# A hybrid decoder step on one core: the expert routing by pairs of heads, and the output projection by blocks of its inputs

## The reference

```python
z = rmsnorm(x, norm1_g) @ w_in                     # 2048 -> 6200
y_a = cb * short_conv(cc * ch)                     # columns    0..511  of the mixer output
y_b = gated sum of three attention branches        # columns  512..1535
y_c = gated, normed mLSTM heads (4 x 128)          # columns 1536..2047
x = x + concat(y_a, y_b, y_c) @ w_out              # 2048 -> 2048
h = rmsnorm(x, norm2_g)
q = (h @ wq).reshape(T, 8, 2, 128)                 # 8 heads, two halves
s = einsum('thcd,hcnd->thcn', q, subkeys)          # 16 sets of 128 scores a row
s1, i1 = top_k(s[:, :, 0], 16); s2, i2 = top_k(s[:, :, 1], 16)
top, pos = top_k(s1[..., :, None] + s2[..., None, :], 16)    # of 256 candidates a head
eidx = i1 * 128 + i2 at pos;  g = softmax(top)
act = gelu(einsum('td,thkd->thk', h, u[eidx]))     # 128 gathered rows of u a token
x = x + einsum('thk,thkd->td', g * act, v[eidx])   # 128 gathered rows of v a token
y = rmsnorm(x, final_norm_g)
```

## Time and profile before

| | |
|---|---|
| median of 3 runs | 3102.96 us (3099.08 to 3103.07) |
| the profiled execution | 3101.28 us, span 3099.5 us |
| busy in the span | PE 1612.3 us (52%), DVE 2002.9 (65%), POOL 1096.2 (35%), ACT 270.3 (9%) |
| mean granted PE clock | 0.707 of full |
| moved by DMA | 992.93 MB, of these 671.13 by gathers |
| gathers, 640 | 10.3 us (u) and 16.3 us (v) from issue to landing, medians |

### The profile page before, as it was taken

One profiled execution on the slowest core, in us unless ns is written; L12 is line 12 of the kernel. 1 busy time (PEld: TensorE's weight loads), 2 busy tenths in 40 slices (PEclk: granted clock), 3 DMA queues, 4 the chain that ended last, 5 costly groups with the idle time before them and its releaser, 6 DMA issues.

```text
span 3099.5 us, 20042 instructions
## 1 busy us (share of the span) xinstructions
PE 1612.3 (52%) x6113; PEld 1010.5 (33%) x6113; DVE 2002.9 (65%) x2607; ACT 270.3 (9%) x590; POOL 1096.2 (35%) x644
## 2 busy tenths in 40 slices
PE   7985956778887756632767667424787000000000
PEld 3454552222224632632545555301277000000000
DVE  0024147766664864663777777676562999999998
ACT  1012101000001200100211111200010000000000
POOL 0000003233440222201334334222430488888885
PEclk9975987899897568766888878755855555555555
DMA  8942748999994669837899999866994599999997
GB/s 275 304 147 82 260 141 317 414 412 412 412 412 139 244 220 394 346 96 285 346 387 387 388 392 401 301 192 216 396 402 196 226 422 422 422 422 422 422 422 320
DMA packets 267343, 992.93 MB, mean 320 GB/s; under 512 B 31218, under 2 KB 60599, under 8 KB 183433
## 3 DMA queue, kind: packets, MB, share of 16 engines
q0 software_dynamic: 92160, 671.13, 53.2%
q1 hardware_dynamic: 174072, 319.40, 29.5%
q10 hardware_dynamic: 1040, 1.59, 0.1%
HBM read 980.73 MB, written 19.77 MB: 323 GB/s over the span
## 4 chain that ended last, share of the span: by engine, by line
PE 36%; DMA 24%; POOL 16%; DVE 13%; issue 5%; SPq 4%; ACT 2%; DVEq 0%; ACTq 0%; POOLq 0%
POOL arena L1584 16%; PE ps L724 10%; DMA arena<-in_w_in_dram 10%; PE ps L865 6%; DMA arena<-in_cache_nsa_kv_dram 6%; PE ps L843 5%; DMA arena<-in_w_out_dram 3%; PE ps L360 2%; DMA arena<-in_peer_wq_dram 2%; SPq L565 2%; SPq L566 2%; PE ps L363 2%; DVE arena L1072 2%; DMA arena<-in_peer_v_dram,arena 2%; DVE arena L1150 1%
## 5 line engine op out<-in xcount | busy, mean ns | idle before, releaser
L1584 POOL DMA_INDIRECT arena<-in_peer_u_dram,arena x320 | 496.7, 1552 | 1373.4 <-DVEq L1533 705.8
L1069 DVE CUSTOM_DVE_ANT_0 arena<-arena 128x2048 bf16<-128x2048 f32 x320 | 733.4, 2292 | 241.5 <-DMA arena<-in_peer_u_dram,arena 183.2
L1584 POOL DMA_INDIRECT arena<-in_peer_v_dram,arena x320 | 599.3, 1873 | 599.4 <-DVE arena L1072 385.2
L1072 DVE SCALAR_TENSOR_TENSOR arena<-arena 128x2048 f32<-128x2048 f32 x296 | 696.0, 2351 | 102.4 <-DMA arena<-in_peer_v_dram,arena 63.5
L724 PE MATMUL ps<-arena 128*128 128x512 f32 (+1 forms) x1152 | 544.7, 629 | 78.9 <-DMA arena<-in_w_in_dram 76.7
L724 PEld LDWEIGHTS ps<-arena 128*128 128x128 f32 (+1 forms) x1152 | 202.4, 183 | 420.0 <-issue 316.9
L865 PE MATMUL ps<-arena 128*128 128x128 f32 (+1 forms) x1536 | 236.3, 334 | 32.7 <-DMA arena<-in_peer_wq_dram 32.7
L865 PEld LDWEIGHTS ps<-arena 128*128 128x128 f32 x1536 | 235.1, 249 | 33.9 <-DMA arena<-in_peer_wq_dram 22.3
L843 PE MATMUL ps<-arena 128*128 128x512 f32 (+1 forms) x384 | 189.7, 656 | 53.5 <-DMA arena<-in_w_out_dram 53.5
L360 PE MATMUL ps<-arena 128*128 128x128 f32 x512 | 74.8, 319 | 193.1 <-DMA arena<-in_cache_nsa_kv_dram 193.1
L360 PEld LDWEIGHTS ps<-arena 128*128 128x128 f32 x512 | 73.3, 234 | 196.0 <-DMA arena<-in_cache_nsa_kv_dram 196.0
(11 more groups left out here) (327 smaller groups left out, 1607.7 us busy)
## 6 DMA issues: line engine op xcount, KB each, us to landing
arena<-in_w_in_dram SPq DMA_DIRECT2D x96, 1024.0 KB, 8.7
arena<-in_w_out_dram SPq DMA_DIRECT2D x48, 1024.0 KB, 10.2
arena<-in_peer_wq_dram SPq DMA_DIRECT2D x48, 1024.0 KB, 5.7
arena<-in_cache_nsa_kv_dram SPq DMA_DIRECT2D x128, 384.0 KB, 9.0
arena<-in_cache_nsa_kv_dram SPq DMA_DIRECT2D x128, 128.0 KB
arena<-in_state_win_kv_dram SPq DMA_DIRECT2D x32, 256.0 KB, 21.7
out_s_win_dram<-in_state_win_kv_dram SPq DMA_DIRECT2D x1, 8064.0 KB
arena<-in_peer_u_dram,arena POOLq DMA_INDIRECT x320, 10.3
```

The source lines that it names most:

```text
L1069: nc.vector.tensor_tensor_reduce(out=PROD, in0=rows_in, in1=H[t], scale=1.0, scalar=0.0, op0=ALU.mult, op1=ALU.add, accum_out=DOTS[:, c:c ...
L1072: nc.vector.scalar_tensor_tensor(out=ACC[t], in0=rows_in, scalar=GG[:, t, c:c + 1], in1=ACC[t], op0=ALU.mult, op1=ALU.add).then_inc(g_used, 1)
L1584: nc.gpsimd.indirect_dma_start(BUF[SLOT[p]], None, tables[kind], bass.IndirectOffsetOnAxis(EIDX[:, t, c:c + 1].bitcast(U32), 0)).then_inc( ...
```

## The change

Two things, in one diff.

**The output projection by blocks of its inputs.** `out_part(n)` multiplies input block `Y_ORDER[n // 4]` (1, 2, 0, 3: attention, attention, convolution, heads) into column block n % 4. All four column blocks stay open in PSUM banks 4 to 7 until the last four parts. In tiles 0 and 1, the two attention blocks of Y are transposed when the attention ends, ACT copies them ahead of the forget gates, and their eight parts are issued two to a head: one behind the score matmuls, one behind the transposes of the weighted scores. SP issues 12 of the 16 loads in that order there, ahead of the stores of the mLSTM memory. Behind the heads stand two blocks' transposes and eight parts. Tile 2 has the new order, with all parts behind the heads. DVE's addition to x of column c now waits for part 12 + c.

**Routing by pairs of heads.** Column block c of the query projection holds two PEER heads, four score sets. The four 128-column groups of a block now share one bank, and one ACT copy takes them. After blocks 1, 2 and 3, PE computes the scores of the pair before (`pair_scores`), the last pair's follow; ACT stores them in two alternating buffers outside RING, and DVE routes each pair by itself (`route_pair`), every step a quarter as wide. In tiles 1 and 2 the 20 gathered rows ahead of the routing become 10, 4, 3 and 3, ahead of each pair. POOL waits for each pair's quarter of the row numbers. `v_cd` now comes after the last pair. Tile 1's and the sample's first norm move into tile 0's query projection and routing. For tile 2 the row numbers and gates of the two halves are laid out in another order.

```diff
+        Y_ORDER = (1, 2, 0, 3)
+        Y_BANK = (2, 3, 0, 1)
 ...
-                for n in range(4):
-                    sp.dma_start(RING[:, n], w_part(w_out, 0, n)).then_inc(w_slot[n], 16)
+                for n in range(12 if t < 2 else 4):
+                    if n >= 4:
+                        sp.wait_ge(w_used, W1[t] + n - 3)
+                    sp.dma_start(RING[:, n % 4], w_part(w_out, n % 4, Y_ORDER[n // 4])).then_inc(w_slot[n % 4], 16)
 ...
+                def out_part(n):
+                    i, c = n // 4, n % 4
+                    pe.wait_ge(a_yt, 4 * t + i + 1)
+                    pe.wait_ge(w_slot[c], 4 * W1[t] + 16 * i + 16)
+                    for j in range(KS):
+                        last = nc.tensor.matmul(ps[0:r, 4 + c, :], XT[:, KS * Y_ORDER[i] + j, 0:r], RING[:, c, j, :],
+                                                start=(i == 0 and j == 0), stop=(i == 3 and j == KS - 1))
+                    last.then_inc(w_used, 1)
+                if t < 2:
+                    pe.wait_ge(v_uy, NU * t + NU)
+                    for i in range(2):
+                        y_transposed(i)
 ...
                     nc.tensor.matmul(ps[0:r, 1, 0:w], MQT[:, h, 0:r], MKT[:, h, 0:w], start=True, stop=True).then_inc(t_gr, 1)
+                    if t < 2:
+                        out_part(2 * h)
                     pe.wait_ge(v_wqk, hh + 1)
 ...
                     last.then_inc(t_mwt, 1)
+                    if t < 2:
+                        out_part(2 * h + 1)
                     pe.wait_ge(a_mwt, hh + 1)
 ...
+                for i in range(2 if t < 2 else 0, 4):
+                    y_transposed(i)
+                for n in range(8 if t < 2 else 0, 16):
+                    out_part(n)
 ...
+                    if c:
+                        pair_scores(c - 1)
+                pair_scores(3)
 ...
+                def scores_out(c):
+                    act.wait_ge(t_sc, 4 * t + c + 1)
+                    if c >= 2:
+                        act.wait_ge(v_route, 4 * t + c - 1)
+                    nc.scalar.copy(SC[c % 2][r], ps[r, 6 + c % 2].rearrange("p (q n) -> p q n", q=4)).then_inc(a_sc, 1)
 ...
-                    dve.wait_ge(w_used, W1[t] + 4 * c + 4)
+                    dve.wait_ge(w_used, W1[t] + 12 + c + 1)
 ...
+                for c in range(4):
+                    if t:
+                        take((10, 4, 3, 3)[c])
+                    dve.wait_ge(a_sc, 4 * t + c + 1)
+                    route_pair(t, c)
+                    if t == 0 and c == 1:
+                        first_mean(1)
+                        first_mean(2)
+                    if t == 0 and c == 2:
+                        first_rstd(1)
+                        first_rstd(2)
 ...
-                if kind == "u" and c == 0:
-                    pool.wait_ge(v_route, t + 1)
+                if kind == "u" and c % (COLS[t] // 4) == 0:
+                    pool.wait_ge(v_route, 4 * t + c // (COLS[t] // 4) + 1)
```

More of the change, by code:

```diff
@@ L993, in _, with yt_stored @@
                     mlstm_qk()
+                def yt_stored(i):
+                    j = Y_ORDER[i]
+                    act.wait_ge(t_y, 4 * t + i + 1)
+                    nc.scalar.copy(XT[:, 4 * j:4 * j + 4, 0:m], ps[:, Y_BANK[i]].rearrange("p (q n) -> p q n", q=4)[:, :, 0:m]).then_inc(a_yt, 1)
+                if t < 2:
+                    for i in range(2):
+                        yt_stored(i)
                 act.wait_ge(v_mf, 2 * t + 1)
```

197 lines of the change are left out of this document (109 added, 88 removed).

## The result

The changed kernel takes 2995.49 us (median of 4 runs, 2993.38 to 3001.14), the kernel before, run beside it, 3101.02 us: ratio 0.9668, 95% interval 0.9644 to 0.9693. In a later series of five runs it took 2999.76 us, ratio 0.9704 (0.9686 to 0.9721). The forecast was 2972 us, with a range of 2940 to 3028. The sign and the range hold. The gain came out 24 us smaller than forecast (105.5 us by the medians instead of 129.5), and the shortfall is not spread evenly.

What follows compares the result with a forecast made beforehand. No single bound: DMA, DVE or PE by stage, and shortening the DVE program ahead of the end's 256 gathers shortens the run. Terms -13 -27 -17 -19.5 -6 +1 -28 -20 = -129.5 against 3101.3 gave 2972 us, range 2940 to 3028.

Steps and rivals of the forecast that it cites:

- Tile 0, heads and projection: Eight parts moved into tile 0's heads add 16 us there and take 29.6 from the projection: net -13 us.
- Tile 0, routing: Pairs of 15.5 us routed beside tile 0's query projection; tile 1's matmuls start at 470 instead of 497.1: -27 us.
- Tile 1, heads and projection: Moved parts add 14.6 us to tile 1's heads; the projection gives 32 (bounds 24 to 38): net -17 us.
- Tile 1, routing: Tile 1's pair 0 starts at 1292.5 after 11 us of idle, routing ends at 1380.4: -19.5 us (bounds -8, -25).
- Tile 2's projection: New order without moved parts, loads at full rate while DVE waits, same bytes: +1 us (-3 to +6).
- Tile 2's routing: Pairs routed beside tile 2's query projection, done at 2413; the end's gathering started at 2441.3 before: -28 us.
- The lead: Eight gathers of the end, issued before pair 3, land in idle DMA: -20 us, down to 0 if DVE takes over.
- A: Rival: the moved parts in the heads of tiles 0 and 1 run at 1.2 GHz, +48.6, 3020 us; chance 0.12.
- B: Rival: gathers keep 3.25 us each and starve the weights; tile 1, lead and sample gain less, 3026 us; chance 0.15.
- C: Rival: more than forecast, pairs at 13.2 us, waits all hidden, all lower bounds together, 2940 us; chance 0.06.
- D: Rival: lower clock from heads to end of query projection in tiles 0 and 1, +160, 3132 us; chance 0.05.
- E: Rival: pairs not routed beside the projection at all, routing terms become +3, +9, +9, 3068 us; chance 0.02.

Runs made afterwards that it cites:

- e9: The changed kernel with w_out by rows in all tiles but all sixteen parts behind the heads, none inside; 3035.39 us, ratio 0.9808.
- e6: The changed kernel with tile 1's twenty gathered rows before the pairs split 4, 6, 5, 5 instead of 10, 4, 3, 3; 3015.77 us, ratio 0.9734.
- e3: The changed kernel with GpSimd holding every gather of a tile until the tile's last pair is routed; 3019.86 us, ratio 0.9769.
- e4: The changed kernel with tile 2's w_out read and multiplied column by column as before; 2985.85 us, ratio 0.9641.
- e7: The changed kernel with tile 2's gathered rows split 17, 1, 1, 1 before the four additions instead of 5, 5, 5, 5; 2985.64 us, ratio 0.9649.

## Why the prediction was right, and where it wasn't

**What bounds the kernel.** "Whatever shortens the one DVE program ahead of that point shortens the run" held: the parts of the change add up, alone and together, and no stage is seen to give back what an earlier one gained.

**Tile 0, heads and projection: -13, measured -14 (e9: the moved parts).** The working holds: a head is 7.7 us without parts and 9.8 to 11.5 with them (head 0: 13.2). Its last step is rounded the wrong way, 16 less 29.6 is -13.6. "I take full clock in tile 0": granted was 0.88 over the four heads, 0.94 in the second profile, with three parts of the eight in one profile and one in the other at 5.1 to 5.4 us. The Trainium skill (TensorE: Matmul & The Clock Gate, HAM oscillation) tells of bursts cut by DMA waits that are longer than the 1.9 us here; the case that the prediction drew from it did not arise, the parts rose to 3.60 us.

**Tile 0, routing: -27, measured -25.** The first search came 31 us behind the norm as forecast, and the pairs 15.9 us apart, where the forecast has 432, 448 and 464. Tile 1's matmuls start at 458.6, forecast about 457.

**Tile 1, heads and projection: -17, measured -18 to -21.** The clock's loss was near the estimate: first parts of 4.9 to 5.4 us and second parts of 3.60, 1.3 to 1.8 us a head where 1.1 were taken. But a head grew by only 2.2 us (11.6 to 13.8), not 3.65, so the second part's 2.55 was priced too high; from the first head to the transposes it is +11, not +14.6. The projection took 70 us from the transposes to the last addition (forecast 69). Eight of the loads had been fetched in the heads, and what was left ran with DMA full (share 0.99, 392 GB/s).

**Tile 1, routing: -19.5, measured -10.3, in its bounds.** The step that failed is "parts 6 and 7 are done by 1291, pair 0 starts at 1292.5". It let the weights have DMA from the moment when VectorE takes its last row. The trace has two waits of 6.23 and 6.83 us of TensorE for `peer_wq` instead, the last after the last row:

```profile
1216.10 5.21 PE L907 MATMUL ps<-arena 128*128 128x128 f32 x32 [6.23 <-DMA arena<-in_peer_wq_dram]
1228.14 5.97 PE L907 MATMUL ps<-arena 128*128 128x128 f32 x32 [6.83 <-DMA arena<-in_peer_wq_dram]
```

GpSimd issues its last gather at 1218.38, as VectorE ends its last row. The buffers freed last are still to be filled then, and DMA stays full without any row being taken:

```profile
1218.00:1236.00 18.00, 11.17 (x76) 10.98 (x76) 0.38 (x3) 1.17 (x2) 0.94 (x1) 0.78 0.97 370
```

In these 18 us 6.7 MB are moved: 2.75 MB for the gathers still open, 3.9 MB for loads, of which four were open at once (the two that TensorE waits for had been issued at 1198.8 and 1202.4 and landed 29 us later). The refill of the buffers, 7.4 us at this rate, is what the forecast left out, and most of the 8.4 us by which pair 0 is late. e6 is the counter-test for the direction (fewer rows, pair 0 16 us earlier) and shows that the same bytes then come between the pairs.

**Sample: -6, measured -5 to -14.** The forecast's reason (4 MB less beside the pages) is seen in the first 31 rows: 6 to 9 us with early gathers, of which 2 to 5 go when e3 holds them back. The rest of the stage scatters by 10 us in kernels with either routing, and why is open; the -14 of one profile is in part luck.

**Tile 2's projection: +1 (-3 to +6), measured +13.** "The bytes are the same" is the step that failed, the only term with stated bounds that came out beyond them. The prediction itself had seen that VectorE would stop gathering and that "loads run at full rate"; it took the rate for DMA's. While no gather goes, the loads run at TensorE's rate, one part in 3.6 us, 319 GB/s in the measured window (e4 and e7, with gathers beside them: 412 and 414). And with `w_out` read out early, SP goes on to `peer_wq`, whose parts then lie beside the 15 gathers that the norm waits for: 2.7 MB more ahead of the norm, and gathers at 3.25 us instead of the 2.5 that they take alone.

**Tile 2's routing: -28, measured -21.** The gap before pair 0 (25.1) and the pace of TensorE at the lower clock (27.57 us for 128 records; 27.5 by the earlier trace rows, 48.05/224 x 128) were right. The largest miss is the three rows ahead of pair 3: 10.2 us with two waits of 1.3 and 1.5, where 7.1 were taken; pair 0 came 58.7 us behind the norm instead of 56.4, and the rest is small. The waits between pairs for TensorE, 3.9 and 6.3 us, were in the forecast in kind. The two waits of 1.3 and 1.5 come from DMA with DMA half busy: the prediction called DMA idle in routing, which it read in tile 1 (0.03), but in tile 2 the copy of the window state runs there. That the copy slows the gathers is read from the traces (29.6 to 31.8 us from issue to landing of the `v` gathers that were issued while it ran, in all ten profiles of the new routing); no run moves the copy.

**The lead: -20, measured -9.** The step that failed is "eight landed ones are worth -20". They are worth 8 x 2.51 = 20.1 us of DMA only if DMA works on from there. Before, the first gather of the end was issued 5.7 us ahead of its first row, so that gathers were already under way; now the ninth is issued 2.6 us behind the first row, as it needs a free buffer. These 8.3 us come off. Another 3 come off as the pipe fills: from the first gather counted to the last row, before 648.3 us = 256 x 2.51 + 5.7, now from the ninth 631.4 = 248 x 2.51 + 8.9. 20.1 - 8.3 - 3.2 = 8.6, the first profile's difference; this is an account of the trace that closes by its making, the test is e3, where the end is back at 645.4 us. The prediction's lower bound was DVE taking over; it didn't (DMA at 1.01, 422 GB/s), the loss was DMA that was busy for about a third of the 12 us from 2338 to 2350.

**The rivals.** A: granted clock 0.88 and 0.94 in tile 0's heads; wrong. B had the right mechanism in the wrong strength: gathers at 3.25 us starving the weights, in tile 1's routing and tile 2's projection, but the end and the moved parts' gain stood. C, D and E are out by the same rows: pairs at 15.8 us, a granted clock of 0.77 and 0.78 in the windows of tile 1's projections (D needs 0.50), pairs beside the projection.

## What to carry to other kernels

In a stage where weights and gathered rows share DMA, ask at each moment who lets the next transfer go. Loads alone went at the matmuls' pace here, below what DMA gives. A consumer put behind a long accumulation stops its own transfers, and the loads of the next stage then slip in ahead of it: the stage gets longer although the kernel moves the same bytes. A lead of prefetched buffers is worth its bytes less the time in which DMA has too little to do once they are all full. With four buffers a fifth row in a stretch can wait, by 0.5 to 9.9 us here, by how full DMA is. And before calling DMA idle in a stage, look at the same stage in each tile.

## What the runs showed of the hardware

A gather issued with DMA full took 16.8 us to the use of its row (issued 1235.3, used 1252.1 in e6); with DMA free, 5.9 us (e3, 2345.77 to 2351.64); beside a copy in packets of 64.5 KB 30.3 us to its landing, though DMA was busy only half of the time (the gather's packets are 8 KB). The same float32 part takes 3.60 us right after another one and 4.9 to 5.4 us behind a wait of 1.9 to 3.4 us in some heads, while behind the same 1.87 us in others it takes 3.60: the waits alone don't decide it. Stages full of paged reads or gathers scatter by 10 us between executions (743 to 755 us, 566 to 577) while tile 2's routing repeats within 2 us and tile 1's within 5, so a change in the first kind needs repeated profiles, or a milestone early in the stage.
